# Two weight tiles kept as one tensor with alternating words: every TensorE weight load reads with a step of two

## The chip, the cores and the metric

The kernel runs on one core of one Trainium2 chip. The metric is the time on the device in microseconds (us). The kernel before took 2760.2 us, the median of three runs (2759.54 to 2764.32). TensorE (PE) multiplies, VectorE (DVE) and ScalarE (ACT) do the work by element, GpSimd (POOL) a part of it, and SyncE (SP) starts the transfers of weights.

## The reference

One inference step of a four-layer encoder for 512 new frames and 64 frames of a running stream, 576 tokens (T) of width 1024 (D) in all. Each layer mixes over time and then applies an MLP with a squared ReLU:

```python
for i in range(DEPTH):                       # 4 layers
    a = rms_norm(h, norm_mix[i])
    # layers 0, 3: stick-breaking attention; 1: short gated convolution; 2: gated linear attention
    h = h + mix(a, w_in, w_out)              # w_in: 1024 x 3072, w_out: 1024 x 1024
    h = h + sq_relu_mlp(rms_norm(h, norm_mlp[i]), w_up, w_down)

def sq_relu_mlp(x, w_up, w_down):            # 1024 x 4096, 4096 x 1024
    h = jax.nn.relu(x @ w_up)
    return (h * h) @ w_down
```

All inputs and outputs are float32. Nearly all the arithmetic lies in the products with the weights.

## The kernel before, in words

The activations stand in SBUF with the features on the 128 partitions and the 576 tokens along the row. A product with a weight matrix is cut into slabs: 1024 rows (8 blocks of 128, index `k`) by 256 columns (2 chunks of 128, index `m`). There are 48 slabs a layer and 192 in all, in one fixed order. Everything is placed by hand: each engine has its own program, and semaphores join them.

A float32 product is made from three products of type float32r. The weight is split in a rounded part `whi` and the rest `wlo`, the activation likewise in `a_hi` and `a_lo`, and `whi*a_hi + whi*a_lo + wlo*a_hi` is summed in PSUM. For each slab `s`, chunk `m` and block `k`, `project` thus issues three pairs of matmuls (the halves `h` of the tokens, 288 columns each), and each matmul comes with a load of its 128 by 128 weights (LDWEIGHTS, shown as PEld). That is 96 loads and 96 matmuls a slab, 18,432 of each at line 395.

A slab's weights pass three engines. SP loads them into `raw[:, u]` (line 342; `u` is 0 or 1 in turn). ScalarE copies them rounded to `whi[:, u]` (`split_next`, line 852; the first slab in line 917), once the last slab that used that half is done. VectorE subtracts, `wlo[:, u] = raw[:, u] - whi[:, u]` (`split`, line 1183). TensorE waits for `w_lo` before the slab. Both splits are done one slab ahead, ahead of the other work of that slab in the programs of ScalarE and VectorE.

The space of `whi` and `wlo` has a second use. `w_f` is the same place seen as one row of 8192 words; in the stick-breaking attention the `u = 1` halves hold the scores (`keep`, `beta`), named `w_f` in the trace.

In the linear attention of layer 2 `LEVELS` (32, 16, 8, 4, 2, 1) names block sizes. At level `half` the lines 1374 and 1386 (VectorE) and the moving operand of line 692 (TensorE) take runs of `half` words and skip `half` words after each, so that at the last of these six levels they take every second word:

```python
v = t.rearrange("p (b s) -> p b s", s=2 * half)
return v[:, :, 0:half], v[:, :, half:2 * half]                     # halves(), lines 307 and 308
q = q.rearrange("p (b s) -> p b s", s=2 * half)[:, :, half:2 * half]   # line 689
```

The levels come one after the other, at each a `right_exponents` (line 1374), a `decayed_queries` (line 1386), and two batches of matmuls of line 692 among the matmuls of a slab.

Of the kernel before, what the change touches and what calls it, by code (L numbers as in the profile page):

```python
# [20 lines left out]
F32R = mybir.dt.float32r  # L21
# [5 lines left out]
P = 128  # L27
# [5 lines left out]
D = 1024  # L33
KC = D // P
# [5 lines left out]
SLAB = 256  # L40
# [44 lines left out]
def trunk(nc, x_prompt, x_sample, cache_sb_k, cache_sb_v, state_conv, state_gla, norm_mix, norm_mlp, sb_w_qkv, sb_w_o,  # L85
          conv_w_in, conv_w, conv_w_out, gla_w_in, gla_w_gk2, gla_b_gk, gla_norm, gla_w_o, mlp_w_up, mlp_w_down,
          norm_final, y_prompt, y_sample, sb_k_p, sb_v_p, sb_k_s, sb_v_s, conv_p, conv_s, gla_p, gla_s):
    with ExitStack() as ctx:
        def sb(name, shape, dt):
            return ctx.enter_context(nc.sbuf_tensor(name, shape, dt))  # L90
# [4 lines left out]
        def passing(name, shape, dt):  # L95

            with nc.sbuf_tensor(name, shape, dt) as t:
                return t
# [20 lines left out]
        tails_t = sb("tails_t", [4 * KC, P], F32)  # L119
        raw = sb("raw", [P, 2, KC, SLAB], F32)  # L120
        w_f = passing("w_f", [P, 8 * D], F32)
        whi = sb("whi", [P, 2, KC, SLAB], F32R)
        wlo = sb("wlo", [P, 2, KC, SLAB], F32R)


        apart = sb("apart", [P, 16], F32)
# [90 lines left out]
        block_mask = stg[:, 4608:5120]  # L217
        KT = flat(0, 8)[:, 0:4 * D].rearrange("p (t f) -> p t f", t=4)
        raw_f = raw[:, :, :, :].rearrange("p u k c -> p (u k c)")
        whi_f, wlo_f = w_f[:, 2 * D:4 * D], w_f[:, 6 * D:8 * D]  # L220

        def keep(u):

# [1651 lines left out]
```

## Time and profile before

| | before |
|---|---|
| median of three runs | 2760.2 us |
| the profiled execution's own time | 2763.89 us |
| its span in the profile | 2762.2 us |
| TensorE matmul busy | 2731.4 us |
| TensorE weight load busy | 2659.4 us |
| VectorE busy | 1266.0 us |
| ScalarE busy | 857.4 us |
| GpSimd busy | 223.2 us |

Busy times of matmul and weight load overlap each other, and consecutive records of one kind overlap too, so a busy share near 100% says that TensorE was never idle for long, and not how fast it went. How fast it went is read from the start times of consecutive instructions.

### The profile page before, as it was taken

To read this page: it belongs to the slowest core of one execution; us is meant where nothing else is said; L and a number is where in the kernel's file an instruction comes from. 1 tells how busy PE (TensorE), PEld (TensorE's weight loads), DVE (VectorE), ACT (ScalarE), POOL (GpSimd) and SP (SyncE) were. 2 spreads that over 40 slices of the span, in tenths; PEclk is the share of its full clock that TensorE was granted. 3 is DMA by queue.
4 is the path that set the end of the run, shared out by engine and by line. 5 is a ranking of instruction groups with operands and counts; after the bars stand their busy time and mean duration, and the time that the engine had idled before them with its cause. 6 is when DMAs were issued, how large, how long until landed. Compare 5 with 4: busy or idle time off the path is not lost.

```text
span 2762.2 us, 48400 instructions
## 1 busy us (share of the span) xinstructions
PE 2731.4 (99%) x20754; PEld 2659.4 (96%) x20754; DVE 1266.0 (46%) x1577; ACT 857.4 (31%) x933; POOL 223.2 (8%) x232
## 2 busy tenths in 40 slices
PE   8999999999999999999999999999999999999998
PEld 8986999999999999999999899999999969999998
DVE  4258534333455434334478543333342494433433
ACT  3147322122312323223224432222331384221222
POOL 4000100000211100000233110000010001000001
PEclk9999999999999999999999999999999999999999
DMA  4211322222222222222212122222222103322221
GB/s 147 88 66 32 111 92 77 92 78 90 77 92 76 77 92 77 91 77 79 90 47 76 40 89 80 89 79 90 78 94 90 47 36 120 98 76 92 76 91 50
DMA packets 205540, 223.64 MB, mean 81 GB/s; under 512 B 3766, under 2 KB 200480, under 8 KB 205392
## 3 DMA queue, kind: packets, MB, share of 16 engines
q1 hardware_dynamic: 200992, 206.06, 23.3%
q0 software_dynamic: 4400, 15.41, 1.6%
q8 instruction: 117, 1.92, 0.3%
q14 instruction: 31, 0.25, 0.0%
HBM read 208.60 MB, written 12.86 MB: 80 GB/s over the span
## 4 chain that ended last, share of the span: by engine, by line
PE 96%; DVE 1%; ACT 1%; issue 0%; DMA 0%; POOL 0%; SPq 0%; ACTq 0%; DVEq 0%
PE bank L395 88%; PE bank L500 2%; PE bank L460 1%; PE bank L521 1%; PE bank L692 1%; PE bank L468 0%; PE bank L560 0%; PE bank L640 0%; PE bank L415 0%; PE bank L747 0%; DMA big<-in_x_prompt 0%; DVE wlo L1183 0%; PE bank L454 0%; DVE e L1288 0%; PE bank L746 0%
## 5 line engine op out<-in xcount | busy, mean ns | idle before, releaser
L395 PE MATMUL bank<-ahi,whi 128*128 128x288 f32 x3584 | 770.0, 295 | 8.2 <-DVE alo L1208 6.8
L395 PE MATMUL bank<-alo,whi 128*128 128x288 f32 x3584 | 766.0, 295 | 0.0
L395 PE MATMUL bank<-ahi,wlo 128*128 128x288 f32 x3584 | 762.8, 294 | 0.0
L852 ACT ACTIVATE whi<-raw 128x2048 fp32r<-128x2048 f32 x191 | 364.4, 1908 | 832.2 <-PE bank L395 825.5
L395 PEld LDWEIGHTS bank<-ahi,whi 128*128 128x128 f32 x3584 | 573.3, 188 | 13.1 <-DVE wlo L1183 7.0
L395 PEld LDWEIGHTS bank<-ahi,wlo 128*128 128x128 f32 x3584 | 575.5, 188 | 0.0
L395 PEld LDWEIGHTS bank<-alo,whi 128*128 128x128 f32 x3584 | 575.5, 188 | 0.0
L395 PE MATMUL bank<-hhi,whi 128*128 128x288 f32 x2560 | 549.0, 295 | 3.8 <-DVE hlo L1544 2.0
L395 PE MATMUL bank<-hlo,whi 128*128 128x288 f32 x2560 | 547.7, 295 | 0.0
L395 PE MATMUL bank<-hhi,wlo 128*128 128x288 f32 x2560 | 545.4, 294 | 0.0
L1183 DVE TENSOR_TENSOR wlo<-raw,whi 128x2048 fp32r<-128x2048 f32 x192 | 444.1, 2313 | 208.7 <-ACT whi L852 206.1
L395 PEld LDWEIGHTS bank<-hhi,whi 128*128 128x128 f32 x2560 | 409.7, 188 | 4.4 <-issue 2.1
L395 PEld LDWEIGHTS bank<-hhi,wlo 128*128 128x128 f32 x2560 | 411.6, 188 | 0.0
L395 PEld LDWEIGHTS bank<-hlo,whi 128*128 128x128 f32 x2560 | 411.2, 188 | 0.0
L1591 DVE TENSOR_TENSOR X<-bank,X 128x288 f32 (+1 forms) x320 | 131.6, 452 | 470.2 <-PE bank L395 470.1
L1145 ACT ACTIVATE big<-big 128x576 f32<-128x576 f32 x128 | 87.8, 686 | 540.9 <-DVE big L1608 540.9
L1608 DVE SCALAR_TENSOR_TENSOR big<-bank,rstd 128x288 f32<-128x288 f32 x256 | 105.3, 453 | 224.3 <-PE bank L395 219.8
L1612 DVE TENSOR_TENSOR hlo<-big,hhi 128x576 f32 (+1 forms) x128 | 97.1, 759 | 182.7 <-ACT hhi L1146 182.7
L1256 DVE TENSOR_TENSOR big<-bank,rstd 128x288 f32<-128x288 f32 x152 | 62.4, 452 | 192.0 <-PE bank L395 191.9
L1684 POOL MEMSET big<- 128x576 f32 x8 | 4.6, 579 | 1602.7 <-PE bank L395 1602.7
L1688 POOL TENSOR_TENSOR big<-big 128x576 f32<-128x576 f32 x63 | 98.1, 1558 | 288.2 <-ACT big L886 288.2
L883 ACT ACTIVATE ahi<-X,vec (+1 forms) x64 | 49.0, 776 | 227.7 <-DVE X L1591 227.6
(247 smaller groups left out, 1514.6 us busy)
## 6 DMA issues: line engine op xcount, KB each, us to landing
raw<-in_mlp_w_up SPq DMA_DIRECT2D x64, 1024.0 KB, 5.4
raw<-in_mlp_w_down SPq DMA_DIRECT2D x64, 1024.0 KB, 5.1
raw<-in_sb_w_qkv SPq DMA_DIRECT2D x24, 1024.0 KB, 5.2
raw<-in_conv_w_in SPq DMA_DIRECT2D x12, 1024.0 KB, 5.2
raw<-in_gla_w_in SPq DMA_DIRECT2D x12, 1024.0 KB, 5.3
raw<-in_sb_w_o SPq DMA_DIRECT2D x8, 1024.0 KB, 5.2
out<-mixs POOLq DMA_DIRECT2D x2, 2048.0 KB, 7.6
out<-big POOLq DMA_DIRECT2D x2, 2048.0 KB, 8.2
```

Source lines behind the costliest of these rows:

```text
L395: mm = pe.matmul(acc[h][:, 0:HALF], w[:, u, k, m * P:(m + 1) * P], a[:, k, h * HALF:(h + 1) * HALF], start=(k == 0 and w is whi and a is a ...
L460: mm = pe.matmul(z[:, places[e]:places[e] + n], big[r, p, P * i:P * i + P], big[r, 8 + p, 0:n], start=False, stop=False, skip_group_check= ...
L500: return pe.transpose(turned_bank[0:rows, at:at + P], a[:, src:src + rows], ident[:])
L852: act.activation(whi[:, 1 - u], raw[:, 1 - u], ACT.Copy).then_inc(w_hi, 1)
L883: act.activation(at(ahi, j), at(X, j), ACT.Copy, scale=g).then_inc(xg_hi, 1)
L1145: act.activation(sq_h[m], relu_t[m], ACT.Square).then_inc(hid_sq, 1)
L1183: dve.tensor_tensor(wlo[:, u], raw[:, u], whi[:, u].bitcast(F32), ALU.subtract).then_inc(w_lo, 1)
L1256: ins = dve.tensor_tensor(dst, acc, rstd[:, hs], ALU.mult)
L1591: ins = dve.tensor_tensor(part(X, j, hs), bank[2 * m + h][:, 0:HALF], part(X, j, hs), ALU.add)
L1608: ins = dve.scalar_tensor_tensor(relu_t[m][:, hs], bank[2 * m + h][:, 0:HALF], 0.0, rstd[:, hs], ALU.max, ALU.mult)
L1612: dve.tensor_tensor(at(hlo, c), sq_h[m], at(hhi, c).bitcast(F32), ALU.subtract).then_inc(hid_ready, 1)
L1688: pool.tensor_tensor(ssq, ssq, sq_x, ALU.add).then_inc(ssq_add, 1)
```

## The change

`whi` and `wlo` were two tensors of 2 x 8 x 256 words a partition. They become the two views of one tensor with an innermost dimension of two, so that a rounded weight and its low part are neighbours in SBUF. No instruction is added, removed or moved, and the programs of SyncE and GpSimd are the same. What differs is the step of four kinds of access: ScalarE's write of `whi`, VectorE's read of `whi` and write of `wlo`, and TensorE's read of its weights, all of which go from neighbouring words to every second word (8 bytes apart). `raw` is read as before. The second hunk follows from the new layout: the `u = 1` half is now the words 4D to 8D of the row, and `whi_f` and `wlo_f` are two parts of it, contiguous as before.

```diff
-        whi = sb("whi", [P, 2, KC, SLAB], F32R)
-        wlo = sb("wlo", [P, 2, KC, SLAB], F32R)
+        weights = sb("weights", [P, 2, KC, SLAB, 2], F32R)
+        whi, wlo = weights[:, :, :, :, 0], weights[:, :, :, :, 1]
...
-        whi_f, wlo_f = w_f[:, 2 * D:4 * D], w_f[:, 6 * D:8 * D]
+        whi_f, wlo_f = w_f[:, 4 * D:6 * D], w_f[:, 6 * D:8 * D]
```

## Rows read from the trace of the kernel before

**Rows 1.** The page: span, and busy time by engine.
```profile
span 2762.2 us, 48400 instructions
PE 2731.4 (99%) x20754; PEld 2659.4 (96%) x20754; DVE 1266.0 (46%) x1577; ACT 857.4 (31%) x933; POOL 223.2 (8%) x232
```

**Rows 2.** The page: shares of the chain that ended last.
```profile
PE 96%; DVE 1%; ACT 1%; issue 0%; DMA 0%; POOL 0%; SPq 0%; ACTq 0%; DVEq 0%
```

**Rows 3.** The page's costliest groups: line, engine, operation, shapes, count, busy us, mean ns.
```profile
L395 PE MATMUL bank<-ahi,whi 128*128 128x288 f32 x3584 | 770.0, 295 | 8.2 <-DVE alo L1208 6.8
...
L852 ACT ACTIVATE whi<-raw 128x2048 fp32r<-128x2048 f32 x191 | 364.4, 1908 | 832.2 <-PE bank L395 825.5
...
L395 PE MATMUL bank<-hhi,whi 128*128 128x288 f32 x2560 | 549.0, 295 | 3.8 <-DVE hlo L1544 2.0
...
L1183 DVE TENSOR_TENSOR wlo<-raw,whi 128x2048 fp32r<-128x2048 f32 x192 | 444.1, 2313 | 208.7 <-ACT whi L852 206.1
```

**Rows 4.** The chain in order of time: start us, length us, what, count.
```profile
329.75 406.20 PE bank L395 x3072
```

**Rows 5.** Line 395 in stretches: length, PE busy, PEld busy, granted clock, DMA share, GB/s.
```profile
19.00:24.00 5.00, 5.00 (x21) 5.00 (x22) 0.50 0.87 311
400.00:700.00 300.00, 300.00 (x2271) 300.00 (x2271) 1.00 0.26 81
```

**Rows 6.** Timeline of PE near 21 us: start us, length us, two matmuls a row.
```profile
21.05 0.68 PE L395 MATMUL bank<-alo,whi 128*128 128x288 f32 x2
...
22.49 0.68 PE L395 MATMUL bank<-alo,whi 128*128 128x288 f32 x2
```

**Rows 7.** Groups of weight loads of line 692, by shape: count, busy us, mean ns.
```profile
L692 PEld LDWEIGHTS bank<-stg 128*128 128x128 f32 x192 | 22.5, 191 | 0.0
L692 PEld LDWEIGHTS bank<-stg 128*64 128x64 f32 x80 | 5.3, 137 | 1.4 <-DVE stg L1404 0.8 <-issue 0.3
```

**Rows 8.** Timeline of PE: a batch at level 16, one at level 1, what follows.
```profile
1432.30 1.89 PE L692 MATMUL bank<-stg 128*128 128x64 f32 x16
1434.00 0.52 PE L395 MATMUL bank<-ahi,whi 128*128 128x288 f32 x2
...
1500.25 1.89 PE L692 MATMUL bank<-stg 128*128 128x64 f32 x16
1501.95 0.51 PE L395 MATMUL bank<-ahi,whi 128*128 128x288 f32 x2
```

**Rows 9.** Timeline of DVE: lines 1374 and 1386 at levels 32 and 1.
```profile
1409.36 1.36 DVE L1374 TENSOR_TENSOR stg<-stg 128x1152 f32<-128x1152 f32 x1
...
1414.93 1.34 DVE L1386 TENSOR_TENSOR stg<-big,stg 128x1152 f32<-128x1152 f32 x1
...
1484.20 1.35 DVE L1374 TENSOR_TENSOR stg<-stg 128x1152 f32<-128x1152 f32 x1
...
1493.74 1.34 DVE L1386 TENSOR_TENSOR stg<-big,stg 128x1152 f32<-128x1152 f32 x1
```

**Rows 10.** Timeline of ACT and DVE in a steady slab of a down projection.
```profile
998.29 1.92 ACT L852 ACTIVATE whi<-raw 128x2048 fp32r<-128x2048 f32 x1 [8.77 <-PE bank L395]
1000.24 2.29 DVE L1183 TENSOR_TENSOR wlo<-raw,whi 128x2048 fp32r<-128x2048 f32 x1 [1.00 <-ACT whi L852]
```

**Rows 11.** Timeline where a split is done closest to its first load.
```profile
274.76 2.29 DVE L1183 TENSOR_TENSOR wlo<-raw,whi 128x2048 fp32r<-128x2048 f32 x1 [3.04 <-ACT whi L852]
...
280.56 0.30 PEld L395 LDWEIGHTS bank<-hhi,whi 128*128 128x128 f32 x2
```

**Rows 12.** Timeline of the start: the first split and the first load.
```profile
15.82 2.29 DVE L1183 TENSOR_TENSOR wlo<-raw,whi 128x2048 fp32r<-128x2048 f32 x1 [2.43 <-ACT whi L917]
18.96 0.29 PEld L395 LDWEIGHTS bank<-ahi,whi 128*128 128x128 f32 x1 [7.00 <-DVE wlo L1183]
```

**Rows 13.** The chain in order of time, in layer 2.
```profile
1414.74 1.91 ACT whi L852
...
1416.68 4.27 DVE wlo L1183
```

## The prediction

> **What bounds the kernel now.** I read the page first. TensorE is busy 2731.4 us of a span of 2762.2 us, and the chain that ended last is 96% TensorE [rows 1, 2]. So the time is the number of matmuls times the distance between the starts of two of them, plus some 4% of waits. The groups give the number: line 395 has six groups of matmuls, three with 3584 and three with 2560, 18,432 in all, and as many weight loads [rows 3]. The chain in order of time gives the distance: a stretch without a gap holds 3072 of them in 406.20 us, 132.2 ns each [rows 4]. 18,432 x 132.2 ns = 2437 us, 88% of the span. The reader is to see that this one distance is the kernel: one nanosecond more on it is 18.4 us, or 0.67%, and 0.3 ns would already be above the 0.2% (5.5 us) that a measurement of this kernel can tell from no change.
>
> Next, what sets the 132.2 ns. A matmul streams 288 columns. The windows show a granted clock of 0.50 from 19 to 24 us and 1.00 from 400 us on, the levels 1.2 and 2.4 GHz [rows 5]. At the low level, six matmuls start in 1.44 us, 240 ns each, which is exactly 288 columns at 1.2 GHz [rows 6]. At the high level 288 columns are 120 ns, and 12.2 ns come on top from something that the trace doesn't name. The weight load beside each matmul is hidden: loads of 128 columns take 191 ns as recorded and loads of 64 columns 137 ns, so 64 columns are worth 54 ns and 128 columns 108 ns, with a fixed part that overlaps the neighbours [rows 7]. Where the moving operand is short, the loads themselves set the distance, and it agrees: a batch of 16 takes from 1432.30 to 1434.00 us, 106 ns each [rows 8]. The load has thus 132 - 108 = 24 ns of cover. If reading every second word costs it less than a fifth of its own rate, TensorE shows nothing; all beyond that stands on the bound, 18,432 times.
>
> **The change part by part.** Nothing is added or moved; four accesses get a step of two words.
>
> *TensorE's weight read.* The trace before has no weight load with a step. Bounds: below, 0 (I exclude a gain from the load, since it is not what sets the distance; a gain in the unexplained 12.2 ns is a rival). Above, half rate: 2 x 108 = 216 ns, 84 ns over the 132. The nearest rows are those of layer 2, where the same engine reads its moving operand with words skipped. At level 1 that is every second word. Its batch of 16 has the same length as that at level 16, 1.89 us, and the next matmul starts 1.70 us after it in both [rows 8]. That is weaker than it looks, as a moving operand of 64 columns has the cover of a 108 ns load. The second nearest rows are VectorE's, on the same memory: line 1386 reads two sources and writes one result, all at every second word at level 1, in 1.34 us as at level 32, and line 1374 takes 1.35 against 1.36 us [rows 9]. That is 1.17 ns a word, nothing hides it, and it is the plain rate, since the split over 2048 neighbouring words takes 2313 / 2048 = 1.13 ns a word [rows 3]. The load asks for a word every 108 / 128 = 0.84 ns, somewhat quicker. Between the ends I take 0: it is nearest to these rows, and the loads run at less than half the rate at which the same engine streams neighbouring words (120 / 288 = 0.42 ns each), so that taking only one word of each neighbouring pair still leaves the load its old rate.
>
> The Trainium skill says the same in another way (SBUF — State Buffer, Specifications (TRN2)): lines of 16 bytes, and full bandwidth as long as a line is hit at least twice, which a step of two float32 words just does. By it the sum is +0.
>
> The Trainium skill's page Vector Engine (DVE) Microarchitecture Reference (5.2 Measured stream behaviour on trn2) speaks against the change: a port keeps its full rate only in runs of at least two adjacent 4-byte words, and its table has up to 2.5 ns a column for small steps. By that the split would take some 5.1 us in place of 2.3 us (an estimate from that page). The rows of level 1 contradict it for a step of two on VectorE [rows 9]; for TensorE's weights no run here shows it yet, and it is what the half-rate rival below rests on as a mechanism.
>
> *VectorE's split* (192 times): reads `whi` and writes `wlo` at every second word. By [rows 9] +0. *ScalarE's copy* (192 times): writes at every second word, 1908 ns for 2048 words [rows 3]; no row shows ScalarE doing that. Bounds: 0 and a doubling, +1.9 us. I take 0, from VectorE's writes. Both lie under cover even if doubled. In a steady slab the copy starts at 998.29 us and the split ends at 1002.53 us [rows 10], while a slab is 96 x 132.2 ns = 12.7 us, so 8 us are free. The closest place is after the attention of layer 0 (and alike in layer 3): the split ends at 277.05 us, its first load is at 280.56 us, 3.5 us of cover [rows 11]. Without cover are the start, where the split ends at 18.11 us and the first load follows at 18.96 us with one small operation between [rows 12], and a few slabs of layer 2 in which copy and split are in the chain [rows 13]. If only the copy doubled: 1.9 us at the start and about three times 1.9 us in layer 2, 7.6 us.
>
> *The second use of the space.* `keep` and `beta` stay contiguous and stay in the `u = 1` half, whose two parts still fill it wholly; waits and order are unchanged. +0.
>
> Sum: 0 on the profiled execution's own 2763.89 us (span 2762.2 us and 1.7 us around it). That execution was 3.7 us above the median, within the three runs shown, so I put the forecast on the median: 2760.2 us.
>
> **The rivals.**
> 1. *The load falls to half rate.* It becomes the bound of each pair: 18,432 x (216 - 132.2) ns = 1545 us, 4305 us. It decides once the load takes over 132 ns. For it: the trace has no load with a step, and 24 ns are a thin cover. Against it: no access with a step of two in the trace is slower. Chance 8%.
> 2. *The load disturbs the stream beside it.* The 12.2 ns at full clock are unexplained and absent at half clock, as if the two reads of TensorE got in each other's way when the stream is fastest. A load now spans twice the memory. If the disturbance grows with that, 12.2 ns more each: 225 us, 2985 us. Against it: the distance is the same in each slab, with no trace of dependence on what else goes on. It counts from 0.3 ns up. Chance 7%.
> 3. *ScalarE or VectorE lose on their writes.* Both doubled are 4.2 us a slab: 4.2 at the start, 0.7 each at the two closest places, 3 x 4.2 in layer 2, about 18 us, 2778 us; the copy alone 2768 us. Chance 5%.
> 4. *Faster.* If the 12.2 ns come from the two reads meeting in neighbouring words and the step undoes some of it, up to 225 us go: 2535 us at the far end, 2742 us for one nanosecond. Nothing in the rows speaks for it. Chance 3%.
>
> My forecast, no change that can be told, has 77%.
>
> **How the numbers follow.** The likeliest is 2760.2 us. The forecast's own range is the scatter of the runs shown with a little to spare, 2755 to 2766. To hold 8 in 10 it takes in rival 3 whole and a small piece of rivals 2 and 4 (half a nanosecond a matmul, 9 us): 2750 to 2785, with some 82% inside. Left out are nearly all of rivals 1, 2 and 4. Faster by over 0.2%: 3%. Within: 77%. Slower: 8 + 7 + 5 = 20%.
>
> **What the profile after would show.** Right: stretches of line 395 alone still at 132.2 ns, weight loads no longer than 191 ns as recorded, the split at about 2313 ns, the copy at about 1908 ns. Rival 1: loads well above 191 ns and distances of 150 to 220 ns. Rival 2: loads hardly longer, and the distance in steady stretches above 132.5 ns. Rival 3: longer copies or splits, an unchanged distance, and waits of TensorE on `weights` at the start and near 1400 us. What would make the forecast wrong is above all that TensorE's weight read isn't like VectorE's reads; that inference from one engine to another is its weakest step.

## The result: 0.74% slower, and the profile after

The changed kernel takes 2782.0 us, the median of four runs (2779.27 to 2782.82), against 2761.26 us before (2759.54 to 2764.32, now four runs): a ratio of 1.0074 with a 95% interval of 1.0062 to 1.0086, some 20.7 us more. That lies in the range that was given, but the forecast of no change was wrong.

The page of the changed kernel, its first lines and the groups that answer to [rows 1] and [rows 3] (`whi` and `wlo` now share the name `weights`, so their groups fall together):

```profile
span 2781.1 us, 48400 instructions
...
PE 2750.9 (99%) x20754; PEld 2679.5 (96%) x20754; DVE 1263.3 (45%) x1577; ACT 891.3 (32%) x933; POOL 224.2 (8%) x232
...
L395 PE MATMUL bank<-ahi,weights 128*128 128x288 f32 x7168 | 1259.1, 298 | 7.1 <-DVE alo L1208 7.1
L395 PEld LDWEIGHTS bank<-ahi,weights 128*128 128x128 f32 x7168 | 1076.2, 197 | 11.8 <-DVE weights L1183 7.2
...
L852 ACT ACTIVATE weights<-raw 128x2048 fp32r<-128x2048 f32 x191 | 398.6, 2087 | 825.9 <-PE bank L395 819.1
...
L1183 DVE TENSOR_TENSOR weights<-raw,weights 128x2048 fp32r<-128x2048 f32 x192 | 444.2, 2314 | 241.9 <-ACT weights L852 239.3
```

The loads of line 395 in the kernel before, from its page:

```profile
L395 PEld LDWEIGHTS bank<-ahi,whi 128*128 128x128 f32 x3584 | 573.3, 188 | 13.1 <-DVE wlo L1183 7.0
```

Three things are to be seen. A weight load of line 395 is recorded with 197 ns in place of 188; the prediction's limit was 191 ns, from the loads of the same shape in line 692 [rows 7]. ScalarE's copy takes 2087 ns in place of 1908, 9% more [rows 3]. VectorE's split, with a step on one source and on its result, takes 2314 ns in place of 2313.

The chain in order of time of the changed kernel gives the distance of two matmuls in a stretch without a gap:

```profile
329.95 409.60 PE bank L395 x3072
```

409.60 us / 3072 = 133.3 ns, against 132.2 ns [rows 4]. The difference, 1.11 ns, times 18,432 is 20.4 us, nearly the whole of the 20.7 us between the medians. (The two profiled executions differ by less, 2781.1 against 2762.2 us of span, since the one before took 1.6 us longer over its first slab; each later slab of line 395 alone is 0.107 us longer in the changed kernel.) The tightest place after the attention of layer 0 [rows 11], in the changed kernel's timeline:

```profile
274.60 2.29 DVE L1183 TENSOR_TENSOR weights<-raw,weights 128x2048 fp32r<-128x2048 f32 x1 [3.21 <-ACT weights L852]
...
280.32 0.32 PEld L395 LDWEIGHTS bank<-hhi,weights 128*128 128x128 f32 x2
```

The split ends at 276.89 us, 3.4 us ahead of its first load, so the slower copy cost nothing here. And at half clock the change costs nothing either. The windows and the timeline of PE in the changed kernel, as in [rows 5, 6]:

```profile
19.00:24.00 5.00, 4.84 (x20) 4.87 (x21) 0.51 0.89 314
400.00:700.00 300.00, 300.00 (x2252) 300.00 (x2251) 1.00 0.25 81
```

```profile
21.22 0.68 PE L395 MATMUL bank<-alo,weights 128*128 128x288 f32 x2
...
22.66 0.68 PE L395 MATMUL bank<-alo,weights 128*128 128x288 f32 x2
```

Six matmuls in 1.44 us, 240 ns each, as before. In the 300 us at full clock 2252 matmuls fit in place of 2271.

### The profile page after: what moved, and what is told of

It is laid out like the page before. It is cut to its first block, busy times and chain, and to the rows that moved or that the text cites. A ratio compares the mean times of both kernels' runs of the same rounds, so it can differ in the third digit from the quotient of the medians.

```text
span 2781.1 us, 48400 instructions
## 1 busy us (share of the span) xinstructions
PE 2750.9 (99%) x20754; PEld 2679.5 (96%) x20754; DVE 1263.3 (45%) x1577; ACT 891.3 (32%) x933; POOL 224.2 (8%) x232
## 4 chain that ended last, share of the span: by engine, by line
PE 97%; DVE 1%; ACT 1%; issue 0%; DMA 0%; POOL 0%; ACTq 0%; DVEq 0%
PE bank L395 88%; PE bank L500 2%; PE bank L460 1%; PE bank L521 1%; PE bank L692 1%; PE bank L468 0%; PE bank L560 0%; PE bank L640 0%; PE bank L415 0%; PE bank L747 0%; DVE weights L1183 0%; PE bank L454 0%; DVE e L1288 0%; PE bank L430 0%; PE bank L746 0%
## 5 line engine op out<-in xcount | busy, mean ns | idle before, releaser
L395 PE MATMUL bank<-ahi,weights 128*128 128x288 f32 x7168 | 1259.1, 298 | 7.1 <-DVE alo L1208 7.1
L395 PEld LDWEIGHTS bank<-ahi,weights 128*128 128x128 f32 x7168 | 1076.2, 197 | 11.8 <-DVE weights L1183 7.2
L395 PE MATMUL bank<-hhi,weights 128*128 128x288 f32 x5120 | 900.7, 298 | 3.8 <-DVE hlo L1544 2.0
L395 PE MATMUL bank<-alo,weights 128*128 128x288 f32 x3584 | 773.9, 298 | 0.0
L395 PEld LDWEIGHTS bank<-hhi,weights 128*128 128x128 f32 x5120 | 769.5, 197 | 4.4 <-issue 2.1
L852 ACT ACTIVATE weights<-raw 128x2048 fp32r<-128x2048 f32 x191 | 398.6, 2087 | 825.9 <-PE bank L395 819.1
L395 PEld LDWEIGHTS bank<-alo,weights 128*128 128x128 f32 x3584 | 591.2, 197 | 0.0
L1183 DVE TENSOR_TENSOR weights<-raw,weights 128x2048 fp32r<-128x2048 f32 x192 | 444.2, 2314 | 241.9 <-ACT weights L852 239.3
L395 PE MATMUL bank<-hlo,weights 128*128 128x288 f32 x2560 | 552.7, 298 | 0.0
L395 PEld LDWEIGHTS bank<-hlo,weights 128*128 128x128 f32 x2560 | 422.9, 197 | 0.0
```

Of the source, the lines that this page charges most:

```text
L395: mm = pe.matmul(acc[h][:, 0:HALF], w[:, u, k, m * P:(m + 1) * P], a[:, k, h * HALF:(h + 1) * HALF], start=(k == 0 and w is whi and a is a ...
L852: act.activation(whi[:, 1 - u], raw[:, 1 - u], ACT.Copy).then_inc(w_hi, 1)
L1183: dve.tensor_tensor(wlo[:, u], raw[:, u], whi[:, u].bitcast(F32), ALU.subtract).then_inc(w_lo, 1)
```

## The experiments

All are the kernel before with one edit, but `write2`, which starts from the changed kernel. In most the products are of permuted or other columns, as the expectations say. The distances are those of the profile: an entry of the chain divided by its count, as above. `read2` was run four times and `write2` ten times, each other experiment once. In the diffs a call that goes over two lines is drawn into one where that is shorter, and the labels behind `#` are added.

**Read or write?** `read2` keeps the two tensors and steps only the loads; `write2` keeps the interleaved tensor and its writes, and loads neighbouring words.

```diff
-  mm = pe.matmul(acc[h][:, 0:HALF], w[:, u, k, m * P:(m + 1) * P],
+  mm = pe.matmul(acc[h][:, 0:HALF], taken(w, u, k, m, 2),             # read2
+  mm = pe.matmul(acc[h][:, 0:HALF], both(u, k, m, w is wlo),          # write2
...
+def taken(w, u, k, m, step):
+    j = 2 * k + m
+    v = w[:, u].rearrange("p k c -> p (k c)")[:, j // step * step * P:(j // step + 1) * step * P]
+    return v.rearrange("p (c s) -> p c s", s=step)[:, :, j % step]
+def both(u, k, m, low):
+    v = weights[:, u, k].rearrange("p c s -> p (c s)")
+    return v[:, (2 * m + low) * P:(2 * m + low + 1) * P]
```

> The kernel before, with two contiguous tensors, in which each weight load of line 395 takes every second word of the 256 columns of its block (chunk m = 0 the even columns, m = 1 the odd ones): the columns of the results are permuted, the amount of work is the same, and no write has a step. Theory A, TensorE's own read with a step of two costs it all: the distance of two matmuls in a steady stretch is 133.3 ns as in the changed kernel (132.2 before), the recorded load 197 ns (188 before), the time some 20 us over before, 2779 to 2783. Theory B, the writes of ScalarE and VectorE with a step disturb TensorE: 132.2 ns, 188 ns, 2758 to 2764.

> The changed kernel, interleaved tensor and writes with a step of two, but each weight load takes 128 neighbouring words of the block (rounded and low words mixed, so the products are others; the amount of work is the same). Theory A: 132.2 ns, load 188 ns, the copy of ScalarE still 2087 ns against 1908 but hidden, 2758 to 2765 us. Theory B: 133.3 ns and 2779 to 2783 us.

`read2` took 2782.37 us, ratio 1.0077 (1.0060 to 1.0094); `write2` 2761.27 us, ratio 1.0001 (0.9991 to 1.0011); before 2760.87 us. The chain and the load of `read2`:

```profile
946.00 409.60 PE bank L401 x3072
```

```profile
L401 PEld LDWEIGHTS bank<-alo,whi 128*128 128x128 f32 x3584 | 590.5, 197 | 0.0
```

and of `write2`, with its copy:

```profile
329.20 406.20 PE bank L400 x3072
```

```profile
L400 PEld LDWEIGHTS bank<-alo,weights 128*128 128x128 f32 x3584 | 574.6, 188 | 0.0
...
L857 ACT ACTIVATE weights<-raw 128x2048 fp32r<-128x2048 f32 x191 | 396.6, 2077 | 818.3 <-PE bank L400 811.1 <-DMA out<-mixs 5.6 <-issue 1.6
```

133.3 and 132.2 ns: TensorE's stepped read makes the whole loss, and the writes make none, though the copy is as slow as in the changed kernel. Theory B is out.

**Larger steps.** `read4`, `read16` and `read3` differ from `read2` by the step alone (in `read3` the last load of a slab also starts further back, so that it stays within the slab).

> As read2, but each load takes every fourth word over two blocks of the slab (columns permuted between chunks and blocks, so the products are others; the same amount of work). Theory A1, the cost goes with the span of memory that a load touches: twice the surplus of a step of two or more, load 205 to 215 ns, distance 134.5 to 136 ns, 2800 to 2830 us. Theory A2, any load whose words aren't neighbours costs the same: 197 ns, 133.3 ns, 2782 us. Theory A3, two words in 16 bytes are still nearly free and one is not: the load gets longer than the stream of 120 ns, distance 150 ns or more, 3100 us or more.

> As read4, with every sixteenth word over the whole slab of 2048 words. Theory A1: far above the run with a step of four, distance 140 ns or more. Theory A2: 133.3 ns, 2782 us. Theory A3: as the run with a step of four, within 2 ns of its distance, since one word in 16 bytes is reached already there.

> The kernel before with loads that take every third word over three blocks (the columns are mixed up; the same amount of work). A load was 111.5 ns alone at a step of one, 118 to 119 at two and 233 at four. If what counts is how many words lie in one line of 16 bytes (4, 2, 1; here 1.33, two of three loads' words standing alone in theirs): 180 to 200 ns. If steps of three still pair up: 133 to 140 ns. If each hop past a pair of words costs in full: 233 ns.

`read4`, `read16` and `read3` took 4620.5, 4449.4 and 3555.5 us. Chain and load group of `read3`, then of `read4`, then of `read16`:

```profile
395.91 538.83 PE bank L402 x3072
```

```profile
L402 PEld LDWEIGHTS bank<-ahi,whi 128*128 128x128 f32 x3584 | 786.7, 263 | 11.0 <-DVE wlo L1190 6.8 <-issue 3.1
```

```profile
485.85 716.70 PE bank L401 x3072
```

```profile
L401 PEld LDWEIGHTS bank<-ahi,wlo 128*128 128x128 f32 x3584 | 1009.2, 330 | 0.0
```

```profile
472.93 687.69 PE bank L401 x3072
```

```profile
L401 PEld LDWEIGHTS bank<-ahi,wlo 128*128 128x128 f32 x3584 | 970.9, 318 | 0.0
```

175.4, 233.3 and 223.9 ns a matmul: here the load is the bound, and theory A3 holds for the step of four. Two figures missed: sixteen was to lie within 2 ns of four and is 9.4 ns below it, and three was to give 180 to 200 ns. Counting groups of four neighbouring words that a load touches, 96 at a step of three and 128 at four, each costs 175.4 / 96 = 1.83 and 233.3 / 128 = 1.82 ns; at sixteen 1.75 ns. So a group isn't of one price throughout. At a step of two it is 64 groups, 117 ns by the price at three and four (an estimate); a contiguous load touches 32, 58 ns by that price, and is held by something else. The Trainium skill (SBUF — State Buffer, Specifications (TRN2)) has lines of 16 bytes with full bandwidth from two hits on. The steps of three and four agree with lines of that size; that two hits are not quite enough for a load is what the next runs show.

**The length of the stream.** `n192`, `n256`, `n320`, `n384` and `n512` change the columns that a matmul streams, with contiguous loads (`_s1`) or a step of two (`_s2`). With 320, 384 and 512 columns the second stream of each pair also starts elsewhere, at token 256, 192 and 64 in place of 288, so that it ends within the row.

```diff
-  mm = pe.matmul(acc[h][:, 0:HALF], w[:, u, k, m * P:(m + 1) * P], a[:, k, h * HALF:(h + 1) * HALF],
+  mm = pe.matmul(acc[h][:, 0:384], w[:, u, k, m * P:(m + 1) * P], a[:, k, h * 192:h * 192 + 384],    # n384_s1
...
+  n = HALF if k == 0 else 192                                                                        # n192_s1
+  mm = pe.matmul(acc[h][:, 0:n], w[:, u, k, m * P:(m + 1) * P], a[:, k, h * HALF:h * HALF + n],
```

> The kernel before with streams of 192 in place of 288 columns in seven of the eight blocks k (a third of those products is left out), loads contiguous. The stream alone is 80 ns, so the load is the longer of the two. Distance: 108 to 112 ns if the 12.2 ns over the stream at 288 columns belong to a full stream, 120 ns (108 + 12) if they belong to each load.

> As n192_s1, each load with a step of two words. Theory L, a load with a step of two is itself some 9 ns longer (197 against 188 ns as recorded) and a long stream hides nearly all of it: here it shows whole, 9 ns over n192_s1. Theory I, the load disturbs the stream beside it and is itself no longer: no more than 1.1 ns over n192_s1.

> The kernel before with streams of 384 in place of 288 columns (the two halves overlap in 192 columns, a third more work; the results aren't used rightly), loads contiguous. The stream alone is 160 ns. Distance 172 ns if the 12.2 ns are a fixed price of each load beside a stream, 176 ns if the stream runs 10% slow over its whole length, 162 ns if a long stream hides what lay open at 288.

> As n384_s1, each load with a step of two words. Theory L: the longer load is hidden by 52 ns of further cover, the same distance as n384_s1 within 0.2 ns. Theory I: 1.1 ns or more over n384_s1, since the load is read while the stream is read, whatever its length.

> The kernel before with streams of 256 in place of 288 columns in seven of the eight blocks k (a ninth of those products is left out), loads contiguous. With the surplus of 12 to 13 ns over the stream that 288 and 384 columns have: 106.7 + 12 = 119 ns. A load alone was 111.5 ns in the run with 192 columns, so 7 ns of cover are left.

> As n256_s1, each load with a step of two words; a load was 118 to 119 ns alone. Theory hard, the distance is the larger of load and stream with its surplus: no more than 0.5 ns over n256_s1, and then the 1.1 ns at 288 columns need another cause. Theory soft, a longer load shows gradually as the cover gets thin: 3 to 5 ns over n256_s1, between the 7 ns at 192 columns and the 1.1 ns at 288.

> The kernel before with streams of 320 columns (the halves overlap in 64 columns, a ninth more work), loads contiguous. Stream 133.3 ns; with a surplus as at 288 and 384 columns 145 to 146 ns.

> As n320_s1, loads with a step of two. Theory soft, what shows depends on the cover left (about 13 ns at 288, 26 ns here, 54 ns at 384): 0 to 0.5 ns over n320_s1. Theory fixed share, some loads are late whatever the cover: 0.8 ns or more over n320_s1; then 384 columns must be special.

> The kernel before with streams of 512 columns (the halves overlap in 448 columns, 78% more work), loads contiguous. Stream 213.3 ns. If the surplus over a stream is a fixed price of each matmul: 225 to 227 ns. If the stream itself runs at about 0.45 ns a column (173.3 / 384) and not at 0.417: 231 ns.

With 192 and 256 columns one block in eight is still 288 wide, so the distance is read between two rows of the timeline of PE, each row two matmuls. `n192_s1` and `n192_s2`, 20 matmuls in 2.23 and in 2.38 us:

```profile
899.88 0.39 PE L396 MATMUL bank<-hlo,whi 128*128 128x192 f32 x2
...
902.11 0.39 PE L396 MATMUL bank<-hhi,wlo 128*128 128x192 f32 x2
```

```profile
899.84 0.40 PE L402 MATMUL bank<-ahi,whi 128*128 128x192 f32 x2
...
902.22 0.40 PE L402 MATMUL bank<-alo,whi 128*128 128x192 f32 x2
```

`n256_s1` and `n256_s2`, 12 matmuls in 1.40 and 22 in 2.64 us:

```profile
900.05 0.40 PE L396 MATMUL bank<-hhi,wlo 128*128 128x256 f32 x2
...
901.45 0.40 PE L396 MATMUL bank<-hhi,wlo 128*128 128x256 f32 x2
```

```profile
899.75 0.40 PE L402 MATMUL bank<-ahi,wlo 128*128 128x256 f32 x2
...
902.39 0.40 PE L402 MATMUL bank<-alo,whi 128*128 128x256 f32 x2
```

The chain of `n320_s1`, `n320_s2`, `n384_s1`, `n384_s2` and `n512_s1`, in this order:

```profile
351.35 450.56 PE bank L395 x3072
```

```profile
354.27 458.75 PE bank L401 x3072
```

```profile
392.49 532.49 PE bank L395 x3072
```

```profile
393.42 532.50 PE bank L401 x3072
```

```profile
481.16 703.16 PE bank L395 x3072
```

| columns | stream alone, columns / 2.4 | distance, contiguous | distance, step of two | surplus of the step | whole time, us |
|---|---|---|---|---|---|
| 192 | 80.0 ns | 111.5 | 119.0 | 7.5 | 2449.1, 2556.3 |
| 256 | 106.7 | 116.7 | 120.0 | 3.3 | 2520.2, 2574.3 |
| 288 | 120.0 | 132.2 | 133.3 | 1.1 | 2760.9, 2782.4 |
| 320 | 133.3 | 146.7 | 149.3 | 2.7 | 3026.5, 3073.3 |
| 384 | 160.0 | 173.3 | 173.3 | 0.0 | 3517.3, 3518.8 |
| 512 | 213.3 | 228.9 | | | 4543.5 |

The row of 288 columns is `before` and `read2`.

At 192 columns the load is the longer of the two, and a step of two makes the distance 7.5 ns longer: theory L is right that the load itself gets slower, 111.5 to 119.0 ns. (Beside 64 columns loads came every 106 ns [rows 8], so 111.5 ns isn't quite a load alone.) The records show it without any stream as well. The first load after the attention of layer 0 comes when no matmul has run for 0.9 us; in the kernel before, in the changed kernel and in `read4` it is recorded with 186, 195 and 308 ns:

```profile
L395 PEld LDWEIGHTS bank<-hhi,whi 128*128 128x128 f32 x1 | 0.2, 186 | 1.0 <-ACT w_f L957 1.0
```

```profile
L395 PEld LDWEIGHTS bank<-hhi,weights 128*128 128x128 f32 x1 | 0.2, 195 | 1.0 <-ACT w_f L957 1.0
```

```profile
L401 PEld LDWEIGHTS bank<-hhi,whi 128*128 128x128 f32 x1 | 0.3, 308 | 1.0 <-ACT w_f L963 1.0
```

The first load of all, at half clock, takes 289, 288 and 309 ns in the same three: there a step of two costs the load nothing.

`n256_s1` was to give 119 ns and gave 116.7; `n256_s2`, at 3.3 ns over it, lay within the 3 to 5 ns of theory soft. But theory L, and my next one that a longer load shows gradually as its cover gets thin, fall with 320 columns: there the cover is larger than at 288, and the surplus is 2.7 ns and not less. The second stream starts at another token there too, so the rise from 1.1 to 2.7 ns may come from the length or from the place; the runs on the place of the stream, below, show that the place counts. At 512 columns the distance is 15.6 ns over the stream, between the 13 of a fixed price and the 18 of a slower stream, so that question wasn't settled.

**One load in three.**

```diff
+  mm = pe.matmul(acc[h][:, 0:HALF], taken(w, u, k, m, 2 if w is wlo else 1),
```

> The kernel before, in which only the loads of wlo (one in three) take every second word (columns of the low products permuted; the same amount of work). If each stepped load pays by itself: a third of 1.1, so 132.6 ns a matmul, 7 us over before. If a late load delays those behind it or they catch up: anything else between 132.2 and 133.3 ns, near 132.2 if the contiguous loads around it make up the time.

The chain of `lo2`:

```profile
944.41 407.90 PE bank L401 x3072
```

132.8 ns (2773.9 us in all, one run), 0.55 ns more: half the loss for a third of the loads, where a third of it (132.6 ns) was named for loads that pay one by one. They neither pay one by one nor are made up for.

**The place of the stream.** `addr_s1` and `addr_s2` keep all lengths and move only the second stream of each pair.

```diff
-  a[:, k, h * HALF:(h + 1) * HALF],
+  a[:, k, 8 * h:8 * h + HALF],
```

> The kernel before, in which the stream of the second half starts 8 tokens after that of the first (h = 1 takes the tokens 8 to 295 in place of 288 to 575; the second half of the results is of other tokens), loads contiguous, 288 columns as before. Theory place, the addresses of stream and load decide how much of a collision shows: a distance other than 132.2 ns by 0.3 ns or more. Theory length, only the lengths do: 132.2 ns.

> As addr_s1, loads with a step of two. Theory place: a surplus over addr_s1 other than 1.1 ns by 0.3 ns or more. Theory length: 133.3 ns, 1.1 ns over addr_s1.

The chain of `addr_s1`, then of `addr_s2`:

```profile
35.73 132.95 PE bank L395 x1008
...
944.74 409.56 PE bank L395 x3072
...
2355.90 379.25 PE bank L395 x2880
```

```profile
328.94 409.61 PE bank L401 x3072
```

They took 2772.8 and 2779.0 us, one run each, beside 2759.7 us of the kernel before. Theory place holds in part. In most stretches of `addr_s1`, as in that from 944.74 us, the distance is 133.3 ns: contiguous loads now pay the 1.1 ns too, with all lengths as they were, only because the stream comes from another place, and there the step adds nothing. Theory length is out. But its first stretch has 132.95 / 1008 = 131.9 ns and the blocks of the last layer 379.25 / 2880 = 131.7 ns, less than before, and the code and the places in memory are the same in the MLP of every layer. So the place alone doesn't fix the distance: with the same places two steady patterns occur, and `addr_s2` is at 133.3 ns throughout.

**The stream with a step.**

```diff
-  a[:, k, h * HALF:(h + 1) * HALF],
+  a[:, k, :].rearrange("p (t e) -> p e t", e=2)[:, h],
```

> The kernel before with contiguous loads and streams of every second token (even tokens for h = 0, odd for h = 1: the tokens of the results are permuted; the same amount of work). A stream asks for a word every 0.42 ns, twice as often as a load. If a step of two halves what a fetch brings: 252 ns a matmul, near 4950 us. If two words a line are enough for the stream as well: 132 to 140 ns.

It took 5051.4 us. The chain of `stream2`:

```profile
523.10 788.47 PE bank L395 x3072
```

256.7 ns a matmul in place of 132.2, near the 252 ns named. A stream with a step of two takes twice as long. It does not follow the clock of TensorE either: at half clock, where the contiguous stream takes 240 ns [rows 6], six matmuls of `stream2` start in 1.55 us, 258 ns each:

```profile
19.41 0.70 PE L395 MATMUL bank<-alo,whi 128*128 128x288 f32 x2
...
20.96 0.69 PE L395 MATMUL bank<-alo,whi 128*128 128x288 f32 x2
```

And its loads, contiguous as before, are recorded with 209 ns in place of 188:

```profile
L395 PEld LDWEIGHTS bank<-alo,whi 128*128 128x128 f32 x3584 | 747.6, 209 | 172.9
```

Where no stream runs, the same kernel's load takes 186 ns, as before. So the load is recorded longer beside such a stream. That is the nearest that a record here comes to showing that TensorE's two reads disturb each other.

## Why the prediction was wrong

**What bounds the kernel** was right: the distance of two matmuls, 18,432 times. The warning beside it, that 0.3 ns would be above the 0.2%, was what happened, with 1.1 ns.

**The step that failed** is that TensorE's weight read costs nothing, and in it this sentence: "If reading every second word costs it less than a fifth of its own rate, TensorE shows nothing". The load did get slower by less than a fifth, 111.5 to 119.0 ns or 7% (`n192_s1`, `n192_s2`), stayed 13 ns short of the 132 ns, and 1.1 ns showed all the same. Load and stream aren't two lengths of which the longer counts. The distance depends on more than the longer length: moving every second stream by 280 tokens costs, in most stretches, as much as stepping all loads (`addr_s1`), 320 columns pay more than 288, and 384 pay nothing. The sum's term for the weight read was 0, and it measured 20.4 us.

**The inference from VectorE** held for VectorE, and not for TensorE, for which it was drawn too. VectorE kept its rate (split 2314 ns), TensorE's load lost 7%, and TensorE's stream, which asks for words twice as fast as the load, lost half (`stream2`). The argument that the load runs at less than half of the stream's rate, and so can do with one word of each pair, was left with no room: `stream2` shows that a stream with a step of two gets a word every 256.7 / 288 = 0.89 ns, and a contiguous load takes one every 111.5 / 128 = 0.87 ns, so the stepped rate is already a little too slow for it. I took it for ample room.

**ScalarE's copy**, taken as 0, is 0.17 to 0.18 us longer (2077 ns in `write2` and 2087 in the changed kernel, against 1908 ns), within its bounds. It is hidden, as the bounds by place said; `write2` has it at no cost that can be told.

**The rivals.** Half rate (rival 1) is what a step of four does, not of two: 233.3 ns in `read4`, where it named 216 for a halved load. Rival 2, that the load disturbs the stream beside it, was of the right kind as far as the runs tell, and had a wrong law: it scaled with the memory that a load spans, 12.2 ns more each, and 1.1 ns were measured; a step of four spans more still, but there the load has become the bound. I gave it 7%, since the distance is the same in each slab. The trace before held only one length of stream for line 395 and one offset between the two streams of a pair, so it couldn't show how the distance depends on either. But it held a sign that more than the longer length counts, in the start times of single matmuls. Over 330 to 730 us the six distances of a block repeat, by mean, as 131.8, 130.0, 132.5, 134.2, 132.5 and 132.5 ns, though all six matmuls and loads are alike in length; at half clock each is 240 ns. From 942 us the same six values sit two matmuls earlier in the block. Rival 3 had no part in it, and rival 4 none.

**The pages.** The rule of the Trainium skill's SBUF — State Buffer page, full bandwidth with two hits in a line, would have left the time as it was. The runs agree in part: a load with two words a line loses 7%, and one with fewer loses far more. For a stream of float32r it doesn't hold: two words a line, and half the rate. The Trainium skill's Vector Engine (DVE) Microarchitecture Reference (5.2 Measured stream behaviour on trn2), which wants adjacent pairs for the full rate, doesn't describe VectorE at a step of two here (2314 ns). A rule of that kind would fit TensorE's stream, of which the page doesn't speak there.

**What stays open.** What decides between 131.7, 132.2 and 133.3 ns, and what makes the 10 to 16 ns that a matmul takes beyond its stream even with contiguous loads. That the two reads fall on each other, and that it matters how they are in step when a stretch begins, is argued from the dependence on the place, from the longer loads of `stream2` and from the two patterns of `addr_s1`; no record names a collision, and no run set the start of a stretch. Whether 320 and 384 columns differ from 288 by their length or by the place of their second stream isn't shown either. For the change itself `write2` and `read2` settle more: TensorE's stepped read is the cause, whatever the mechanism beneath it.

## What to carry to other kernels

Where two operations overlap, a price below the cover isn't a price of nothing: when the distance is paid 18,432 times, ask what a nanosecond costs, and forecast the small loss. In this kernel, with streams of 288 columns, a weight load in float32r had its step of two for under 1% of the time; with other lengths the distance grew by 0 to 3% (256 to 384 columns), and by 7% where the load was the bound (192). A step of four makes the load more than twice as long, and the streamed operand should stay contiguous, since a step of two there nearly doubles its time. A rate seen on one engine at 1.1 ns a word said nothing on operands that ask for one every 0.87 or 0.42 ns.

## What the runs showed of the hardware that was not expected

- The distance of matmuls depends on where the streamed operand lies: 132.2 ns before, and 133.3 or 131.7 ns with nothing but the start of every second stream changed, the loads contiguous (`addr_s1`). Which of the two it is differs between stretches of the same code, and stays so through a stretch.
- The cost of a load with a step of two is not ordered by the stream's length: 3.3, 1.1, 2.7 and 0.0 ns at 256, 288, 320 and 384 columns (at 320 and 384 the second stream also starts at another token).
- At 288 columns the distances come in even steps: six matmuls take 790.1 ns (`addr_s1`, last layer), 793.4 (before), 796.7 (`lo2`) or 800.0 (the changed kernel), 3.3 ns apart. Nothing here shows why.
- A stream with a step of two takes 257 ns at full clock and 258 at half clock, and makes the contiguous loads beside it longer, 209 against 188 ns (`stream2`).
- A load with a step of sixteen words is quicker than one with four, 223.9 against 233.3 ns.
- ScalarE loses 9% when it writes every second word (1908 to 2087 ns for 2048 words); VectorE loses nothing when it reads and writes so.
